# Seven products for a second unit of the down projection, two of its weight sums on GpSimd

## The reference, cut to what matters

```python
u = jnp.einsum('bsd,df->bsf', rms_norm(x, g_mlp[l]), w_up[l])              # 2048 -> 8192
x = x + jnp.einsum('bsf,fd->bsd', jnp.square(jax.nn.relu(u)), w_down[l])   # 8192 -> 2048
return rms_norm(x, g_final)
```

## Time and profile before

| | before |
|---|---|
| median of 3 runs | 1203.43 us (1203.41 to 1203.7) |
| the profiled execution's own time | 1203.42 us |
| its span in the trace | 1201.6 us |
| granted TensorE clock, mean | 0.998 of full speed |
| PE / DVE / ACT / POOL busy | 98% / 71% / 52% / 15% |

### The profile page before, as it was taken

The page is one execution under the profiler, slowest core; times in us unless marked ns, Lnnn a source line. Parts: engine busy times, 40 slices in busy tenths (PEclk is TensorE's granted clock), DMA queues, the critical chain, the costliest instruction groups (busy, mean ns, idle before and its releaser), DMA issues.

```text
span 1201.6 us, 19272 instructions
## 1 busy us (share of the span) xinstructions
PE 1182.1 (98%) x6776; PEld 1035.6 (86%) x6776; DVE 853.1 (71%) x1149; ACT 628.7 (52%) x927; POOL 177.8 (15%) x177
## 2 busy tenths in 40 slices
PE   9999999999999999999999999999999999999996
PEld 7888899999989889888788888788888888888885
DVE  5758766786668867676887666877767787666554
ACT  6445455555645657555544555544655454555442
POOL 2907400030322404200000000000000000000341
PEclk9999999999999999999999999999999999999999
DMA  9674553443644543456456454547543746555531
GB/s 357 252 260 173 196 175 140 162 154 140 246 162 165 181 159 142 151 198 209 166 176 253 175 181 168 210 149 271 175 176 139 264 157 220 191 182 187 198 140 70
DMA packets 51455, 224.43 MB, mean 187 GB/s; under 512 B 3792, under 2 KB 4176, under 8 KB 31696
## 3 DMA queue, kind: packets, MB, share of 16 engines
q1 hardware_dynamic: 50688, 220.22, 50.8%
q10 hardware_dynamic: 720, 3.59, 0.8%
HBM read 221.69 MB, written 2.10 MB: 186 GB/s over the span
## 4 chain that ended last, share of the span: by engine, by line
PE 93%; DVE 3%; ACT 1%; issue 1%; POOL 1%; DMA 1%; SPq 0%; DVEq 0%; ACTq 0%; POOLq 0%
PE bank L1301 16%; PE bank L1298 16%; PE bank L1299 15%; PE extra L1557 6%; PE extra L1559 5%; PE extra L1558 5%; PE bank L1303 4%; PE bank L1305 4%; PE bank L1304 4%; PE bank L1344 3%; PE bank L1346 3%; PE bank L1345 3%; DVE w_low L813 1%; PE bank L1570 1%; PE bank L1571 1%
## 5 line engine op out<-in xcount | busy, mean ns | idle before, releaser
L813 DVE TENSOR_TENSOR w_low<-staged,w_high 128x1024 fp32r<-128x1024 f32 x311 | 390.0, 1269 | 145.5 <-ACT w_high L433 134.9
L433 ACT ACTIVATE w_high<-staged 128x1024 fp32r<-128x1024 f32 x304 | 314.6, 1053 | 189.8 <-PE bank L1301 81.2
L1299 PEld LDWEIGHTS bank<-part_a,w_low 128*128 128x128 f32 x1408 | 264.6, 188 | 61.4
L1298 PE MATMUL bank<-part_a,w_high 128*128 128x512 f32 x704 | 281.0, 399 | 0.0
L1301 PE MATMUL bank<-part_a,w_high 128*128 128x512 f32 x704 | 278.5, 396 | 0.0
L1299 PE MATMUL bank<-part_a,w_low 128*128 128x256 f32 x1408 | 276.8, 278 | 0.0
L719 ACT ACTIVATE w_high<-staged 128x1024 fp32r<-128x1024 f32 x114 | 118.9, 1058 | 108.9 <-PE extra L1559 92.0
L1133 DVE TENSOR_TENSOR w_low<-staged,w_high 128x1024 fp32r<-128x1024 f32 x114 | 137.4, 1221 | 33.8 <-ACT w_high L719 32.6
L361 POOL TENSOR_TENSOR squares<-x 128x256 f32<-128x256 f32 (+1 forms) x31 | 37.3, 1204 | 685.2 <-DVE x L1257 661.3
L1298 PEld LDWEIGHTS bank<-part_a,w_high 128*128 128x128 f32 x704 | 133.7, 190 | 0.6 <-DVE w_low L813 0.3
L1301 PEld LDWEIGHTS bank<-part_a,w_high 128*128 128x128 f32 x704 | 132.0, 187 | 0.0
(11 more groups left out here) (201 smaller groups left out, 1775.1 us busy)
## 6 DMA issues: line engine op xcount, KB each, us to landing
staged<-in_wup SPq DMA_DIRECT2D x64, 1024.0 KB, 4.8
staged<-in_wdown SPq DMA_DIRECT2D x64, 1024.0 KB, 5.0
staged<-in_wqk SPq DMA_DIRECT2D x32, 1024.0 KB, 4.8
staged<-in_wv SPq DMA_DIRECT2D x12, 1024.0 KB, 5.4
staged<-in_wbc SPq DMA_DIRECT2D x8, 1024.0 KB, 4.8
staged<-in_wmk SPq DMA_DIRECT2D x4, 1024.0 KB, 4.7
staged<-in_woa SPq DMA_DIRECT2D x4, 1024.0 KB, 4.8
staged<-in_wcq SPq DMA_DIRECT2D x4, 1024.0 KB, 4.8
```

Of the source, the lines that this page charges most:

```text
L433: nc.scalar.activation(w_high[:, job % 2, cols], staged[:, job % 4, cols], ACT.Copy).then_inc(high_ready, 1)
L813: tt(w_low[:, job % 2, cols], staged[:, job % 4, cols], f32(w_high[:, job % 2, cols]), ALU.subtract).then_inc(low_ready, 1)
L1298: mm(out[:, :], high, both, start=first, stop=False)
L1299: last = mm(out[:, 0:T], low, part[:, slot(kt), 0, :], start=False, stop=False)
```

## The change

- Unit 2 of each group is done by seven products too; units 1 and 3 stay plain. A group now counts 24 halves: 0 to 2 plain blocks of unit 0, 3 to 6 unit 1, 7 to 10 sums of unit 0, 12 to 14 plain blocks of unit 2, 15 and 16 half of unit 3, 17 to 20 sums of unit 2, 22 and 23 the rest of unit 3 (10 and 20 count double).
- Of the four weight sums of a unit, GpSimd makes two (b12-b11 and b22-b12, 128x1024 each), after the low part of b11 is made and both slots have landed; VectorE makes the other two.
- The two units' products accumulate in the same banks, one bank a product. After a group, four additions of 128x1024 (`step`) add the banks to running sums `y`, kept per product bank; the combination of the seven products is made once, in the first eight up jobs of the last quarter (`combine`, six additions per group). ScalarE's copy is gone.
- `y` is twice as large (`y_right` beside `values`); GpSimd clears both parts, and VectorE waits for both.
- Token sums for four pairs per quarter in place of two.
- Loads: unit 0 of group 1 waits for the low parts of the sums of unit 2 (`at - 2` for both slots), the first up loads of the next quarter likewise.
- At the end of the up jobs the halves 2 and 3 of group 0 are made before the last up result is handled.
- The product with ones for the norms of x1 and x2 goes from after job 0 to the middle of the first half of job 1.
- `y` is transposed in the last eight up jobs of the last quarter, four tiles at a time.

```diff
-GROUP_HALVES = 20
-GROUP_STEPS = 12
+GROUP_HALVES = 24
+GROUP_STEPS = 4
-H_SUMS, H_B, H_C = 7, 12, 16
+H_S1, H_RA, H_T1, H_S2, H_RB, H_T2, H_RB_END = 0, 3, 7, 12, 15, 17, 22
...
+                    load_unit(q, g, 0, SLOT_S1[g], (at - 2, at - 2) if g else (at - 6, at - 4))
+                    load_unit(q, g, 1, SLOT_RA[g], (at - GROUP_HALVES + H_RB + 2, at) if g else (at - 2, at))
+                    load_unit(q, g, 2, SLOT_S2[g], (at + H_RA + 2, at + H_RA + 4))
+                    load_unit(q, g, 3, SLOT_RB[g], (at + H_S2, at + H_S2))
...
-            nc.gpsimd.memset(y[:, :, :], 0.0).then_inc(y_clear, 1)
+            nc.gpsimd.memset(y[0], 0.0).then_inc(y_clear, 1)
+            nc.gpsimd.memset(y[1], 0.0).then_inc(y_clear, 1)
+
+            def one_sums(q, g, first, slot, use):
+                b11, b12, b22 = by_pair(slot, 0), by_pair(slot + 1, 0), by_pair(slot + 1, 1)
+                pool.wait_ge(landed[slot + 1], q * 128 + 16 * (JOB_MLP // 4 + 4 + use + 1))
+                pool.wait_ge(low_ready, down_half(q, g) + (first + 1))
+                nc.gpsimd.tensor_tensor(b11, b12, b11, ALU.subtract).then_inc(one_sum_made, 1)
+                nc.gpsimd.tensor_tensor(b12, b22, b12, ALU.subtract).then_inc(one_sum_made, 1)
+
+            with pool.Fori(0, SUMMED_QUARTERS) as q:
+                for g in range(2):
+                    one_sums(q, g, H_S1, SLOT_S1[g], 2 * g)
+                    one_sums(q, g, H_S2, SLOT_S2[g], 2 * g + 1)
...
             def step(q, g, n):
+                pair = (banks_all, extras_all)[n // 2][:, n % 2 * 2:n % 2 * 2 + 2, :]
+                to = y[g][:, 2 * n:2 * n + 2, :]
+                dve.wait_ge(half_done, down_half(q, g) + (H_T2 + 1, H_T2 + 3, H_RB_END, GROUP_HALVES)[n])
+                tt(to, to, pair, ALU.add).then_inc(y_step, 1)
 
             def down_group(q, g, ahead):
+                first, ra, second, rb = SLOT_S1[g], SLOT_RA[g], SLOT_S2[g], SLOT_RB[g]
+                r_tile(q, g, H_RA + 1, ra, 1)
+                r_tile(q, g, H_RA + 2, ra, 2)
+                sum_of_weights(q, first, 2 * g, 2)
+                r_tile(q, g, H_RA + 3, ra, 3)
+                sum_of_weights(q, first, 2 * g, 3)
                 for n in range(4):
+                    s_sum(q, g, H_T1, first, n)
+                s_tile(q, g, H_S2, second, 0)
+                s_tile(q, g, H_S2, second, 1)
+                s_tile(q, g, H_S2, second, 2)
+                r_tile(q, g, H_RB, rb, 0)
+                r_tile(q, g, H_RB + 1, rb, 1)
+                sum_of_weights(q, second, 2 * g + 1, 2)
+                s_sum(q, g, H_T2, second, 0)
+                sum_of_weights(q, second, 2 * g + 1, 3)
+                for n in range(1, 4):
+                    s_sum(q, g, H_T2, second, n)
+                r_tile(q, g, H_RB_END, rb, 2)
                 step(q, g, 0)
+                r_tile(q, g, H_RB_END + 1, rb, 3)
                 step(q, g, 1)
+                ahead(0)
                 step(q, g, 2)
+                ahead(1)
+                ahead(2)
                 step(q, g, 3)
                 ahead(3)
...
-            dve.wait_ge(y_clear, 1)
+            dve.wait_ge(y_clear, 2)
...
             def down_group(q, g):
+                s_products(q, g, H_S1, 0, True)
                 for n in range(4):
+                    r_half(q, g, H_RA + n, n, 1)
+                s_sum_products(q, g, H_T1, 0, True)
+                s_products(q, g, H_S2, 2, False)
+                for n in range(2):
+                    r_half(q, g, H_RB + n, n, 3)
+                s_sum_products(q, g, H_T2, 2, False)
+                for n in range(2, 4):
+                    r_half(q, g, H_RB_END + n - 2, n, 3)
 
             for s in range(4):
-                up(0, 0, s, x2_low if s == 0 else None)
-                if s == 0:
-                    norm_sum(N_X2, extra[3])
+                up(0, 0, s, x2_low if s == 0 else None, N_X2 if s == 1 else None)
```

More of the change, by code:

```diff
@@ L307, in _, with load_up @@
             stream(wco_in, JOB_CO, CROSS)
-            def load_up(q):
-                with sp.Fori(0, QUARTER // 4) as i:
+            def load_up(q, first):
+                if first:
+                    for s in range(4):
+                        load(wup_in[q * 16 + s, :, :], mlp(q), JOB_MLP + s)
+                else:
+                    for s, free in enumerate((-2, -2, H_RB + 2 - GROUP_HALVES, 0)):
+                        sp.wait_ge(low_ready, mlp(q)(2) + (H_MLP + free))
+                        sp.dma_start(staged[:, s, :], wup_in[q * 16 + s, :, :]).then_inc(landed[s], 16)
+                with sp.Fori(1, QUARTER // 4) as i:
                     for s in range(4):
@@ L1282, in half_job @@
             def half_job(off, job, half, out, part, tiles, count=8, total=KT, place=0, wide=True,
-                         slot=lambda kt: kt, waits={}):
+                         slot=lambda kt: kt, waits={}, between=None):
                 pe.wait_ge(low_ready, off(2) + (2 * job + half + 1))
                 for n in range(count):
+                    if between is not None and n == count // 2:
+                        norm_sum(between, extra[3])
                     if n in waits:
@@ L1306, in half_job, with job_of @@
                 return last
-            def job_of(off, job, n_out, part, ready=None, wide=True, slot=lambda kt: kt):
+            def job_of(off, job, n_out, part, ready=None, wide=True, slot=lambda kt: kt, between=None):
                 pe.wait_ge(taken, off(1) + (n_out + 1))
@@ L1317, in job_of @@
                     half_job(off, job, half, bank[job % 4], part, 8 * half, wide=wide,
-                             slot=slot, waits=waits).then_inc(half_done, 1)
+                             slot=slot, waits=waits, between=None if half else between).then_inc(half_done, 1)
             def short_jobs(job, n_out, part, at, waits={}):
@@ L1537, in _, with up, r_half @@
                        {h: (taken, BANKS + OUT_CR + h + 1) for h in range(CROSS)})
[L1539 to L1543 removed]
+            def up(q, i, s, ready=None, between=None):
+                job_of(mlp(q, i), JOB_MLP + s, OUT_MLP + s, part_a, ready, between=between)
+            def r_half(q, g, h, n, unit):
                 at = down_half(q, g)
[L1546 to L1547 removed]
+                slot, cols = half_slot(h)
+                pe.wait_ge(low_ready, at + (h + 1))
                 pe.wait_ge(hid_low, q * 16 + (1 + 4 * unit + n % 2 * 2 + 2))
```

352 lines of the change are left out of this document (165 added, 187 removed).

## The result

| | before | after |
|---|---|---|
| median | 1203.54 us | 1252.91 us (4 runs, 1249.92 to 1254.37) |
| ratio, 95% interval | | 1.0407 [1.0388, 1.0426] |
| span of the profiled execution | 1201.6 us | 1248.1 us |
| granted TensorE clock, mean | 0.998 | 0.983 |

The change makes the kernel 4.1% slower. The forecast was 1248.0 us, its range 1208 to 1262.

A forecast was written before the change was run, and what follows sets the result against it. TensorE's own work was taken as the bound, with VectorE next. 1203.4 us + 42.4 for three quarters (+14.1 each) + 3.5 for the clear - 1.0 for the norm = 1248, range 1208 to 1262.

The forecast's parts named there:

- Rival (a): GpSimd's sums fall into VectorE's pauses, or the port is given back within an instruction: nearly 1211 to 1228 us; chance 0.13.
- (b): No exclusion between VectorE and GpSimd, but late low parts, 5.2 us a quarter: 1209.6 us; chance 0.07.
- (c): Faster: GpSimd's sums wait for VectorE's pauses in plain halves; under 4 us a quarter of holes, 1194 with none; chance 0.10.
- Rival (d): The GpSimd sum is dearer, 3.5 us, as its four strips are not one run: 1268 us; chance 0.08.
- the forecast's own range: Range of the main forecast without the rivals, 1239 to 1258 us; chance 0.62.
- A GpSimd sum: One GpSimd subtract of 1024 columns: 2.65 us, bounds 2.44 to 2.92, shutting VectorE out for about 2.55 of it.
- Unit 2, 8.8 a quarter: In each group's unit 2, GpSimd's two sums delay halves 14 and 15 by 2.2 us each: 4.4 a group.
- Start of group 1, 7.9: Per quarter: half 0 late by 2.0 us through the loads' landing, half 1 by 2.6, half 2 by 3.3.
- Start of group 0, 1.4: Sums fall in the last up jobs, where VectorE idles; 0 to 2.6 us a quarter comes through, 1.4 taken.
- The clear, +3.5: VectorE's wait for the clear of `y` has no slack, so a second clear adds 3.5 us once.
- the norm, -1.0: TensorE's hole at the norm of x1 goes: idle 0.88 us, 1.0 taken as the gain.
- the best case of the change: Fewer matmuls and the hole before half 3, 3 x 3.95 us, plus 1.0 at the norm of x1: 12.9 us.

The follow-up runs named there:

- The best version of it that was run: The changed kernel with all four weight sums on VectorE, the clears waited for late and the landing waited for slot by slot: 1212.12 us, 1.0075 against the kernel before.
- the small parts: Kernel before with half 3 made before the last up result, both norm products in the middle of job 1, the clear waited for late: 1201.53 us, 0.9984.
- an order of VectorE's list that the change did not contain: Kernel before with half 3, norms and clear changed likewise, plus group 0's half 4 low part before VectorE's weight sums, alternating after: 1197.44 us, 0.9949.

## Why the prediction was right, and where its terms were off

The mechanism was the forecast's: VectorE and GpSimd exclude each other over the operands in SBUF, the low parts come late, and TensorE waits. Without the sums 37.6 of 49.4 us are gone, and 39.4 with writes in place of reads; with the reads alone in the kernel before, 23.5 come. Rival (a), sums that fall into pauses, is refuted by the pair of low parts in 5.80 us; (b), no exclusion, by the low parts of 3.41 us; (c) by its own bound, as 16 to 19 us a quarter are left and not under 4. Rival (d) had the sum dearer than it is. Two of its sums are slightly off and change nothing: the terms of (b) add up to 5.0 a quarter and not 5.2, and the forecast's own range would begin at 1238 and not 1239.

- **A GpSimd sum.** Taken as 2.65 us, with 2.44 as the lowest; it is 2.38, below the lower bound. The bound from below took the fixed part four times; with it once, by the prediction's own 0.09, it would be 4 x 0.61 - 3 x 0.09 = 2.17. The value of 2.65 had it once and is still 0.27 too high, and why the rows for 256 columns overstate a longer sum stays open. The Trainium skill ("GPSIMD Engine Reference", 3.1 Elementwise) has 4497 ns for 2048 columns, an estimate of 2.25 for 1024, nearer than mine. Yet the sum made with that estimate, 1238, was further from the result, because the shorter holds were offset by a term that was missing, below.
- **Unit 2, 8.8 a quarter.** Measured 2 x (2.0 + 1.8) = 7.6. The prediction had GpSimd asking just too late, behind half 13's low part, and halves 14 and 15 late. The step that was off is the 0.2 us from the end of half 12's low part to GpSimd's start: it took less than 0.1, and the gap ahead of half 13's low part is 0.13. So GpSimd got in one low part earlier, and the late halves are 13 and 14. How many are late was right, which ones was wrong, and each costs 0.3 less as the sum is shorter. A margin of 0.05 us decides which.
- **Start of group 1, 7.9.** Measured 2.2, 2.2 and 3.2: 7.6. Step 3 behind two late low parts was foreseen. The landing was taken at 2.0; alone it is 2.1.
- **Start of group 0, 1.4.** Measured 0.6, in one wait before half 3 (L1596, three times, 0.5 the longest). The value was inside its bounds, but its reason, idle VectorE time in the up jobs, does not hold in general: eight subtracts a quarter put there cost 7.4 us of an up part. Where the sums went is in the trace: in quarter 1 both run from 760.83 to 765.79, ahead of half 1's low part, and hold two short instructions of an up result's chain, 1.86 and 1.63 us for 0.42 each. The later one:

```profile
764.45 1.63 DVE L1127 TENSOR_TENSOR part_b<-hidden,part_b 128x256 fp32r<-128x256 f32 x1 [0.94 <-ACT part_b L727]
```

In the kernel before with GpSimd's reads, where half 3's low part came behind that result, the same pair cost 1.5 us at this place. Why only 0.6 shows in the change was not tried by itself.
- **The clear, +3.5, and the norm, -1.0.** +2.5 forecast, +3.2 measured. The holes at both norm products went; the MLP starts 1.4 us earlier (479.6 against 481.05), of which 1.2 fall behind 380 us, where the norm of x1 is. But the wait for the clear showed as a hole of 3.8 us, and the half after it ran at half the clock: 5.06 us for what takes 2.79.
- **What was missing: the clock.** By the terms above, read in quarter 1, a quarter has 15.8 us of holes (7.6 + 7.6 + 0.6). Quarter 1 took 16.5 more than 85.8 - 2.7 - 1.25, quarters 0 and 2 took 19.4. The last stretch of group 1, behind its last late half, shows it (quarter 0, then quarter 1):

```profile
655.97:676.79 20.82, 20.14 (x78) 16.10 (x78) 15.01 (x14) 7.47 (x8) 0.00 (x0) 0.89 0.37 147
846.58:864.40 17.82, 17.82 (x78) 14.71 (x79) 15.70 (x14) 8.02 (x8) 0.00 (x0) 1.00 0.39 155
```

The same 78 matmuls take 3.0 us longer at a granted clock of 0.89; TensorE is idle for 0.7 of it, the rest is the clock. In quarter 1 the clock fell as well, but at the start of group 1:

```profile
814.00:822.00 8.00, 5.71 (x12) 3.53 (x12) 8.00 (x5) 3.64 (x4) 5.69 (x2) 0.57 0.29 106
```

There TensorE had to wait for the low parts of halves 1 and 2 anyway, and the slow matmuls filled a part of that wait. What a fall of the clock costs depends on where it comes. The sum had 18.1 us of holes a quarter, 2.3 too many, and no term for the clock; the two nearly cancel, so a part of the agreement (+43.2 against +42.4) is luck. Of the 4.9 us between 1248.0 and 1252.91, 3.0 are the distance from the profiled execution to the median.

The prediction took the best case of the change as 12.9 us. The best version of it that was run is about 9 us slower than before: seven products for a second unit don't pay here even with GpSimd out of it, at least in the order tried. What paid were the small parts (1.9 us), and three times as much together with an order of VectorE's list that the change did not contain (6.1 us).

## What to carry to other kernels

Before moving an elementwise instruction from VectorE to GpSimd, look at what VectorE reads meanwhile: where both read SBUF, and VectorE has two operands there, the move cost more than it freed (1.57 us each here, against 0.44 on VectorE). Idle time of an engine is full cover only if nothing waits at its end; look in the timeline for whether the pause is a link of a chain. A hole that is filled by moving an instruction forward often reappears one place on, so read what the queue of the moved-past engine holds next.

## What the runs showed of the hardware

- A GpSimd sum that waits behind a low part gets in ahead of VectorE's next one, though that stands back to back, in all nine second sums of a pair away from the up jobs. It then holds VectorE for its whole duration: 2.38 us for 1024 columns, of which a low part shows 2.2. A GpSimd clear of the same tile holds it for nothing (0.96 us, beside low parts of 1.22), and a step with one operand in PSUM isn't held (1.21 us beside a sum).
- The granted TensorE clock was 0.50 (1.2 GHz) from 814.2 to 821.0 us and from 1002.0 to 1015.5, right behind a wait of 2.1 us ahead of group 1, and from 653.8 to 660.6, behind the first late half of unit 2 (2.0 us); none of these waits is over 2.2 us. It rose again each time. Beyond their holes the quarters took 0.7 to 3.6 us. Holes alone don't bring it down every time: in the kernel before with GpSimd's reads, quarter 1 had holes of up to 2.6 us and a granted clock of 1.00.
- The runs spread by 4.5 us after and by 0.3 before. That the holes cause this is not shown: the kernel before with GpSimd's reads is 23.5 us slower and spreads by 0.3 too.
